# Input projection: x of chunks 1 to 3 read with channels on partitions and normed there, in place of transposes

## The reference

```python
x = layer_norm(x, ln0_g, ln0_b)         # over the 1024 channels of a frame
h = x @ w_in                            # 1024 -> 1408
a_val, a_gate = h[..., :384], h[..., 384:768]
p_in, q = h[..., 768:1152], h[..., 1152:]
a = a_val * jax.nn.sigmoid(a_gate)      # then a causal depthwise convolution of width 31
p = pool_mixer(p_in)                    # trailing means over 2, 4, 8, 16 frames
mo = memory_cross_attention(q, mem)
x = layer_norm(ALPHA * x + concat(a, p, mo) @ w_out, ln1_g, ln1_b)
```

## Time and profile before

| | us |
|---|---|
| Median of 3 runs | 1891.85 |
| Lowest and highest run | 1891.42, 1892.68 |
| The profiled execution | 1893.02 |
| its span in the trace | 1891.2 |
| TensorE busy in the span | 1844.0 |
| VectorE busy | 1503.3 |
| ScalarE busy | 935.3 |

### The profile page before, as it was taken

The page is one execution under the profiler, slowest core; times in us unless marked ns, Lnnn a source line. Parts: engine busy times, 40 slices in busy tenths (PEclk is TensorE's granted clock), DMA queues, the critical chain, the costliest instruction groups (busy, mean ns, idle before and its releaser), DMA issues.

```text
span 1891.2 us, 26166 instructions
## 1 busy us (share of the span) xinstructions
PE 1844.0 (98%) x8700; PEld 1537.0 (81%) x8700; DVE 1503.3 (79%) x1998; ACT 935.3 (49%) x1585; POOL 174.8 (9%) x250
## 2 busy tenths in 40 slices
PE   7999999999999999999999999999999999999998
PEld 7888888878887788888888788888888787888886
DVE  6636387899998888888888888787878868567999
ACT  3211125676665665656557665655557335325231
POOL 1201010000001022222220020000000000000111
PEclk9999999999999999999999999999999999999999
DMA  6533355444537434343436333122225658557543
GB/s 234 190 111 115 90 163 190 147 153 142 184 133 264 172 123 151 126 145 132 144 133 207 121 129 117 72 89 78 89 78 173 234 199 303 198 172 271 202 170 120
DMA packets 178074, 296.13 MB, mean 157 GB/s; under 512 B 11728, under 2 KB 112336, under 8 KB 178000
## 3 DMA queue, kind: packets, MB, share of 16 engines
q1 hardware_dynamic: 178000, 295.18, 45.1%
HBM read 189.19 MB, written 105.91 MB: 156 GB/s over the span
## 4 chain that ended last, share of the span: by engine, by line
PE 70%; DVE 9%; DMA 2%; ACT 2%; issue 2%; SPq 0%; POOL 0%; DVEq 0%; ACTq 0%; POOLq 0%
PE banks L2268 19%; PE banks L2265 19%; PE banks L2262 19%; PE banks L1199 6%; DVE mov_lo L2482 3%; DVE sta_lo L2478 1%; PE banks L1228 1%; DMA mov_raw<-x_operands 1%; PE banks L1181 1%; DVE up_and_out L2516 1%; DVE up_and_out L2513 1%; PE banks L1132 1%; PE banks L1152 1%; PE banks L1212 1%; PE banks L1263 1%
## 5 line engine op out<-in xcount | busy, mean ns | idle before, releaser
L2262 PE MATMUL banks<-mov_hi,sta_hi 128*128 128x512 f32 x1848 | 499.1, 391 | 6.7 <-ACT half_sums L2352 2.0
L2268 PE MATMUL banks<-mov_lo,sta_hi 128*128 128x512 f32 x1848 | 498.7, 390 | 4.0 <-DVE mov_lo L2482 3.6
L2265 PE MATMUL banks<-mov_hi,sta_lo 128*128 128x512 f32 x1848 | 497.7, 390 | 2.5 <-DVE sta_lo L2478 2.4
L2262 PEld LDWEIGHTS banks<-mov_hi,sta_hi 128*128 128x128 f32 x1848 | 346.4, 188 | 83.9 <-ACT half_sums L2352 3.6
L2268 PEld LDWEIGHTS banks<-mov_lo,sta_hi 128*128 128x128 f32 x1848 | 346.6, 188 | 80.1 <-DVE mov_lo L2482 8.6
L2265 PEld LDWEIGHTS banks<-mov_hi,sta_lo 128*128 128x128 f32 x1848 | 347.2, 188 | 76.3 <-DVE sta_lo L2478 4.1
L2332 ACT ACTIVATE sta_hi<-sta_raw 128x512 fp32r<-128x512 f32 (+1 forms) x340 | 197.7, 611 | 129.9 <-PE banks L2268 94.5
L2478 DVE TENSOR_TENSOR sta_lo<-sta_raw,sta_hi 128x512 fp32r<-128x512 f32 (+1 forms) x340 | 223.8, 673 | 34.6 <-ACT sta_hi L2332 32.7
L2361 ACT ACTIVATE half_sums<-banks 128x512 f32<-128x512 f32 x68 | 40.7, 598 | 175.9 <-PE banks L2268 175.9
L360 PE MATMUL banks<-x0t_hi,win_hi 128*128 128x512 f32 x320 | 126.5, 395 | 0.0
L360 PE MATMUL banks<-x0t_hi,win_lo 128*128 128x512 f32 x320 | 124.8, 390 | 0.0
(11 more groups left out here) (256 smaller groups left out, 2621.4 us busy)
## 6 DMA issues: line engine op xcount, KB each, us to landing
sta_raw<-in_w_up SPq DMA_DIRECT2D x88, 512.0 KB, 4.1
hidden_scratch<-up_and_out SPq DMA_DIRECT2D x44, 512.0 KB, 2.6
y_scratch<-up_and_out SPq DMA_DIRECT2D x16, 1024.0 KB, 7.3
sta_raw<-hidden_scratch SPq DMA_DIRECT2D x32, 512.0 KB, 4.6
up_and_out<-y_scratch SPq DMA_DIRECT2D x16, 1024.0 KB, 4.9
x_operands<-x_operands_out SPq DMA_DIRECT2D x56, 256.0 KB, 4.2
mov_raw<-x_operands SPq DMA_DIRECT2D x14, 1024.0 KB, 8.3
mov_raw<-in_w_down SPq DMA_DIRECT2D x44, 256.0 KB, 4.6
```

The source lines that it names most:

```text
L2262: pe.matmul(psum, sa_hi[j][:, k, :], mv_hi[j][:, k, :], start=(start and k == 0), stop=False, skip_group_check=True)
L2265: pe.matmul(psum, sa_lo[j][:, k, :], mv_hi[j][:, k, :], start=False, stop=False, skip_group_check=True)
L2268: last = pe.matmul(psum, sa_hi[j][:, k, :], mv_lo[j][:, k, :], start=False, stop=(stop and k == m - 1), skip_group_check=True)
```

## The change

Only chunk 0 is transposed on the chip. A second copy of x, `xT`, with channels first and frames in the kernel's order, is given to the kernel as an input. For chunks 1 to 3:

- Each tile is still loaded, normed with frames on partitions and stored. The mean and the root of each of its frames (two numbers, now side by side in columns 12 and 13 of the statistics) are stored too, to a new DRAM tensor of 2048 x 2 (`store_rows`).
- `load_turned` reads half `b` (four blocks of 128 channels) of the chunk from `xT`, 1 MB, into the buffer of the low part.
- When the four tiles of the chunk are stored, `load_rows` reads their 512 pairs back, spread to all 128 partitions.
- `normalise_turned`: VectorE subtracts the means and multiplies by the roots, each on 128 x 2048, in place. The second operand is repeated over the four blocks and steps by two words.
- `affine_hi`: ScalarE applies gain and shift, which are one number per partition here, block by block, and then rounds the half to the high part. It stands behind the evacuation of tiles 7 and 8 in chunk 0, 3 and 4 in chunk 1, 1 and 2 in chunk 2.
- `turned_lo`: VectorE subtracts the high part from the half in place.
- The first projection tile of a chunk waits for the low part of each half when it comes to it.

Slots of x are used in another order: after chunk 0 slot 3 holds the spread rows, and the other five go round. Tiles 4 to 6 are loaded right behind the weights; the loads, stores, norms and pool steps behind them are put in another order, with two more buffers for the pooling. SP waits for the stores of the first pooled half ahead of the load of the taps.

```diff
+    FIRST = 2 * TT
+    SLOTS = (0, 1, 2, 4, 5)
...
+    def slot_of(n):
+
+        return n if n < TT else SLOTS[(n - TT) % len(SLOTS)]
+
...
+    def splits(c, b):
+
+        return FIRST + 2 * (c - 1) + b + 1
...
+        xt_raw = [at("xT_rows0", 118784, [P, KT, CH]), at("xT_rows1", 49152, [P, KT, CH])]
...
+        gb_cols = at("ln0_gb_columns", 212672, [P, 2, KT])
+        row_stats = at("ln0_row_stats", 192512, [P, CH, 2])
...
-                if n in (4, 5):
+                slot = slot_of(n)
+                if n >= TT and slot >= TT and uses(n) == 1:
                     sp.wait_ge(win_lo, len(pieces))
-                if n >= RING:
-                    sp.wait_ge(x0_stored[n % RING], 16 * (n // RING))
-                    sp.wait_ge(tp_ready, 2 * (n - RING) + 2)
+                if uses(n) > 1:
+                    sp.wait_ge(x0_stored[slot], stores(slot, n - 1))
+                if slot < TT and uses(n) == 2:
+                    sp.wait_ge(tp_ready, 2 * slot + 2)
                 rows = a["x"][(n // 8) * HALF:(n // 8 + 1) * HALF, :].rearrange("(q r) d -> r q d", r=PHASES)[n % 8]
-                sp.dma_start(x0[:, n % RING, :], rows).then_inc(x_loaded[n % RING], 16)
+                sp.dma_start(x0[:, slot, :], rows).then_inc(x_loaded[slot], 16)
+
+            def load_turned(c, b):
+                if c >= 2:
+                    sp.wait_ge(proj, JT * (c - 1))
+                src = a["xT"][4 * b * P:4 * (b + 1) * P, c * CH:(c + 1) * CH].rearrange("(k p) t -> p k t", p=P)
+                sp.dma_start(xt_raw[c % 2][:, 4 * b:4 * b + 4, :], src).then_inc(xt_loaded[b], 16)
+
+            def store_rows(n):
+                sp.wait_ge(ln_rstd, n + 1)
+                sp.dma_start(rows_d[n * P:(n + 1) * P, :], st[:, n % RING, 12:14]).then_inc(x0_stored[slot_of(n)], 16)
+
+            def store_tile(n):
+                store_rows(n)
+                store_x0(n)
+
+            def load_rows(c):
+                for u in range(TT):
+                    n = c * TT + u
+                    sp.wait_ge(x0_stored[slot_of(n)], stores(slot_of(n), n))
+                if c == 1:
+                    sp.wait_ge(x0_stored[TT - 1], 16)
+                    sp.wait_ge(tp_ready, FIRST)
+                else:
+                    sp.wait_ge(xt_scaled, 2 * (c - 1))
+                src = rows_d[c * CH:(c + 1) * CH, :].rearrange("(o t) s -> o (t s)", o=1).to_broadcast((P, 2 * CH))
+                sp.dma_start(row_stats[:, :, :].rearrange("p t s -> p (t s)"), src).then_inc(rows_loaded, 16)
...
             load_x(4)
             load_x(5)
             load_x(6)
-            load_x(7)
+            for i, name in enumerate(("ln0_g_columns", "ln0_b_columns")):
+                sp.dma_start(gb_cols[:, i, :], a[name]).then_inc(cols_loaded, 16)
+            load_turned(1, 0)
+            load_turned(1, 1)
...
+                        sp.wait_ge(s, stored_of(i))
+                    sp.wait_ge(tp_ready, FIRST)
+                    sp.wait_ge(xt_scaled, 2 * (NCH - 1))
+                    for s in pooled_out:
+                        sp.wait_ge(s, 16)
...
+                if c == 0:
+                    store_tile(4)
+                    load_x(9)
+                    store_tile(5)
+                    load_x(10)
+                    store_gated(0, 0)
+                    load_x(7)
+                    load_x(8)
+                    store_tile(6)
+                    load_x(11)
+                    store_tile(7)
+                    load_rows(1)
+                    load_x(12)
+                    store_gated(0, 1)
+                    store_gated(0, 2)
+                    store_tile(8)
+                    load_x(13)
+                if c == 1:
+                    load_turned(2, 0)
+                    load_turned(2, 1)
+                    store_tile(9)
+                    load_x(14)
+                    store_tile(10)
+                    load_x(15)
+                    store_gated(1, 0)
+                    store_tile(11)
+                    load_rows(2)
+                    store_gated(1, 1)
+                    store_gated(1, 2)
+                    for n in range(12, 16):
+                        store_tile(n)
+                    load_rows(3)
                 if c == 2:
+                    load_turned(3, 0)
+                    load_turned(3, 1)
                     load_pool(0, 0)
-                for t in range(CT):
-                    store_x0((c + 1) * TT + t)
-                    store_gated(c, t)
-                    if c == 2 and t < 2:
-                        store_pooled(0, t)
-                        load_pool(0, t + 1)
-                store_x0((c + 1) * TT + 3)
-                if c + 2 < NCH:
-                    for u in range(TT):
-                        load_x((c + 2) * TT + u)
-                if c == 2:
+                    load_pool(0, 1)
+                    store_gated(2, 0)
+                    store_pooled(0, 0)
+                    load_pool(0, 2)
+                    store_gated(2, 1)
+                    store_pooled(0, 1)
+                    load_pool(0, 3)
+                    store_gated(2, 2)
                     store_pooled(0, 2)
-                    load_pool(0, 3)
                     store_pooled(0, 3)
...
-                pool.tensor_tensor(s[:, 14:15], s[:, 13:14], half[:, 0:1], ALU.pow).then_inc(ln_rstd, 1)
+                pool.tensor_tensor(s[:, 13:14], s[:, 13:14], half[:, 0:1], ALU.pow).then_inc(ln_rstd, 1)
...
-                if done == c * JT:
-                    pe.wait_ge(lo_done, 2 * TT * (c + 1))
+                if done == 4:
+                    pe.wait_ge(lo_done, FIRST)
...
+                    if c and done == c * JT and k % 4 == 0:
+                        pe.wait_ge(lo_done, splits(c, k // 4))
...
-                    for i in turns_behind(c, n):
-                        turn(c + 1, i)
...
+            def affine_hi(c, b):
+
+                n = 2 * (c - 1) + b + 1
+                act.wait_ge(xt_scaled, n)
+                act.wait_ge(cols_loaded, 32)
+                x = xt_raw[c % 2]
+                for k in range(4 * b, 4 * b + 4):
+                    last = act.activation(x[:, k, :], x[:, k, :], ACT.Identity, bias=gb_cols[:, 1, k:k + 1], scale=gb_cols[:, 0, k:k + 1])
+                last.then_inc(xt_affine, 1)
+                act.wait_ge(xt_affine, n)
                 if c >= 2:
                     act.wait_ge(proj, JT * (c - 1))
-                act.activation(xt_hi[c % 2][:, 4 * b:4 * b + 4, u * P:(u + 1) * P], turned(c, i).rearrange("p (k t) -> p k t", k=4), ACT.Copy).then_inc(hi_done, 1)
+                act.activation(xt_hi[c % 2][:, 4 * b:4 * b + 4, :], x[:, 4 * b:4 * b + 4, :], ACT.Copy).then_inc(hi_done, 1)
...
-                    for i in turns_behind(c, n):
-                        split_hi(c + 1, i)
+                    if c + 1 < NCH:
+                        for b in range(2):
+                            if n == (7, 3, 1)[c] + b:
+                                affine_hi(c + 1, b)
...
-                dve.scalar_tensor_tensor(out=x, in0=x, scalar=s[:, 14:15], in1=g_b[:, 1, :], op0=ALU.mult, op1=ALU.add).then_inc(x0_ready, 1)
-
-            def split_lo(c, i):
+                dve.scalar_tensor_tensor(out=x, in0=x, scalar=s[:, 13:14], in1=g_b[:, 1, :], op0=ALU.mult, op1=ALU.add).then_inc(x0_ready, 1)
...
+            def row_of(i):
+
+                return row_stats[:, :, i].rearrange("p (o t) -> p o t", o=1).to_broadcast((P, 4, CH))
+
+            def normalise_turned(c, b):
+
+                n = 2 * (c - 1) + b + 1
+                x = xt_raw[c % 2][:, 4 * b:4 * b + 4, :]
+                dve.wait_ge(xt_loaded[b], 16 * c)
+                dve.wait_ge(rows_loaded, 16 * c)
+                dve.tensor_tensor(x, x, row_of(0), ALU.subtract).then_inc(xt_centred, 1)
+                dve.wait_ge(xt_centred, n)
+                dve.tensor_tensor(x, x, row_of(1), ALU.mult).then_inc(xt_scaled, 1)
+
+            def turned_lo(c, b):
+                dve.wait_ge(hi_done, splits(c, b))
+                part = (slice(None), slice(4 * b, 4 * b + 4), slice(None))
+                dve.tensor_tensor(xt_lo[c % 2][part], xt_raw[c % 2][part], xt_hi[c % 2][part].bitcast(F32), ALU.subtract).then_inc(lo_done, 1)
...
             for c in range(NCH):
                 if c == 0:
+                    norms(1, 0)
                     gate(0, 0)
+                    norms(1, 1)
                     for i in range(7, 10):
                         weights_lo(i)
-                    norms(1, 0)
-                    norms(1, 1)
-                    lows(1, 0, 1)
+                    norms(1, 2)
                     gate(0, 1)
-                    norms(1, 2)
-                    lows(1, 2, 3)
                     gate(0, 2)
                     norms(1, 3)
-                    lows(1, 4, 5, 6, 7)
-                    continue
+                    norms(2, 0)
+                    for b in range(2):
+                        normalise_turned(1, b)
```

(81 more changed lines are left out.)

118 lines of the change are left out of this document (52 added, 66 removed).

## The result

The changed kernel takes 1900.01 us (median of 5 runs, 1897.63 to 1901.53) against 1891.85: a ratio of 1.0036, 95% interval 1.0025 to 1.0047. It is slower, by about 8 us. I had predicted 1888.8 us and a range of 1884.5 to 1894.0, so the forecast is wrong, in sign and in size. The profiled execution took 1901.53 us, span 1899.8.

A forecast was written before the change was run, and what follows sets the result against it. TensorE's stream was taken as the bound: +4.2 (chunk 1 starting later) - 7.8 (transposes for chunks 2 and 3) + 0.5 (clock) = -3.1 us, giving 1888.8 us, -0.16%; range 1884.5 to 1894.0.

The forecast's parts named there:

- the one on DRAM: Chunk 1's way through DRAM: tile 7 ready at 67.1, store 2.7 us, spread 3.8, with issue rows at 73.8.
- from the rows to the first tile: Chunk 1: from rows at 73.8 through norming, affine and low parts to the first projection tile's end at 94.2.
- its own terms: Range terms: tile 4's bounds (-1.8, +1.7), the transfers (-0.8, +2), the clock (-0.5, +2).
- Rival 3: Chunk 1: tile 7 comes 5.3 us late behind stores of 5.6 us in a full queue; sum +2.2, 1894; chance 0.14.
- Some 20 us of slack each: Chunks 2 and 3: low parts end by 129 and 175, TensorE asks at about 148 and 208; 7.8 us kept.
- The 3.6 us of chunk 0: Transposes removed from four projection tiles of chunk 0: 25.36 us become 21.76, so it ends at 81.0.
- the 7.74 behind chunk 1's first tile: Transposes for chunks 2 and 3 removed from TensorE: 3.9 + 3.9 = 7.8 us gained.
- Rival 2: normalise_turned's stepped operand is read at half rate, 4.5 us per operation, not 2.3: +4.2, 1896; chance 0.08.
- The clock: TensorE's 4.7 us wait at chunk 1 most likely drops its clock to about 0.50, 1.2 GHz; costs 0.5 us.
- the second wait: TensorE's wait for chunk 1's second low half, 88.4 to 91.5; a slow first half, to 90.8, is hidden by it.

The follow-up runs named there:

- e1: Changed kernel without the stores of row statistics, the spread loading the same 4 KB from vector g: 1891.93 us, 0.9993 of the kernel before.
- e3: Changed kernel with each 1 KB row store written as 2 pieces of 512 bytes, from g: 1892.67 us, 0.9997 of the kernel before.
- n1: Order of e2, spread of e1, row stores of 128 pieces of 512 bytes from g: 1890.88 us, 0.9989 of the kernel before.
- n2: Order of e2, spread of e1, row stores of 128 pieces of 64 bytes from g: 1890.33 us, 0.9983 of the kernel before.
- e2: Changed kernel with only SyncE's order in chunk 0 moved, tiles 7 and 8 loaded earlier, 11 later: 1892.03 us, 0.9993 of the kernel before.
- e4: Changed kernel with the edits of e1 and e2 together: 1887.35 us, 0.9973 of the kernel before.
- g2: Changed kernel with chunk 1's rows spread by TensorE, statistics of tiles 5 to 7 and loads of 7 and 8 early: 1904.09 us, 1.0055 of the kernel before.
- g3: Changed kernel, still through DRAM, with tiles 5 to 7's statistics and 8-byte row stores early, tile 7 loaded first: 1906.25 us, 1.0073 of the kernel before.
- g1: Order of e2, spread of e1, 8-byte row stores ahead of the tiles' stores on a semaphore no load waits for: 1893.81 us, 1.0002 of the kernel before.
- h2: Kernel e2 with the 8-byte row stores issued by ScalarE on its own queue, with own semaphores: 1891.83 us, 0.9994 of the kernel before.
- h3: Kernel e2 with each 8-byte row store behind its tile's store, on a semaphore only the spread waits for: 1893.54 us, 1.0000 of the kernel before.

## Why the prediction was wrong

**The step that failed** is the one on DRAM: "The store of tile 7 (the row statistics go out ahead of it, covered by its last norm steps) takes 2.7 us", and with it "At 2.7 us a store tile 7 lands about 62, just before VectorE asks for it at 62.5. I count no delay". I priced the row stores at nothing, by the moment at which they are issued, and took the tile's store from an empty queue. From the trace after: tile 7 is normed 5.7 us late (72.8 for 67.1), its store goes out 1.9 later still, because SyncE stands at the load of tile 11 (I had 0.2 for all issuing, so +1.7), the store takes 7.3 for 2.7 (+4.6), and the spread 5.0 with its issue for 3.8 (+1.2). That makes up the 13.2 us by which the rows are late; from the rows to the first tile it is 20.2 us, forecast 20.4. e1, e3, n1 and n2 show that the stores in 8-byte pieces make the store of a tile slow, e2 that SyncE's order adds to it, e4 that nothing else was missing for chunk 1. By what means 8-byte pieces do this stays open. The range could not have held this: its own terms, added to 1888.8, give 1885.7 to 1894.5 (not quite the 1884.5 to 1894.0 stated), with 2 us for all transfers.

**Rival 3** named the right place and its wait (5.3 us forecast, 5.78 measured), with the wrong cause, a full queue, which is the smaller part: in e1, which keeps the loads, VectorE waits 1.36 us for tile 7. That its number came out is in part luck: the two stores held SyncE for 6.1 and 7.3 us, not 5.6 each. It let only the tile's lateness count and not the slow store of tile 7 itself, so it stopped at 1894.

**A rule I didn't weigh.** The Trainium skill (DMA: Bandwidth & Descriptors, Specifications) puts the least size for full rate at 512 bytes and says that smaller transfers are read, modified and written; it speaks against this change. The runs agree in so far as stores in 8-byte pieces cost (6.2 us for the store of tile 7 in e2 against 3.1 in e4); at 64 bytes, also below that size, they show no such cost (3.1 in n2), and no run here shows the reading and writing back. By that rule the store of tile 7 would not have been priced from rows of large transfers alone.

**"Some 20 us of slack each"** was wrong for chunk 2 by the same step: its rows were forecast at 111 and came at 138. (Chunk 3's were forecast by 158; VectorE began them at 189.6, when their xT had landed, and TensorE did not wait.) g2 shows that chunk 2 then costs a wait of 10.8 us as soon as chunk 1 is on time. So making chunk 1 early, with the row stores of chunk 2 left as they are, would not have saved the change (g2, g3).

**What held.** The 3.6 us of chunk 0 (TensorE's wait begins at 99.0 - 18.0 = 81.0, as forecast) and the 7.74 behind chunk 1's first tile. Rival 2 is false: 2.29 us for an operand with a step of two words. The Trainium skill (SBUF — State Buffer, Door 1: The DMA port swizzle) had it so, and the trace agrees. The clock: 0.56 on average over TensorE's wait, 0.50 at 102 to 103, which is 1.2 GHz, and back at 1.00 at 104. As forecast, the slow half tile hid the second wait: 12 matmuls took 5.1 us, from 99.0 to 104.1, when the second low half was done (101.82 + 2.29). In e4, where TensorE waited 5.1 us, close to the 4.7 of the prediction, the granted clock was 0.50 too from 84 to 90, and 0.2 us were left of the second wait.

## What to carry to other kernels

A transfer of 1 KB in 8-byte pieces was not small here: don't price such a one at nothing for its few bytes, look at the size of its pieces and at what else is moving then. Where a queue's next entry waits for a landing, price every store by the slowest landing in that stretch, not by one from an empty queue. When a chain is mended, follow the same mechanism into the next stage before counting the gain; a delay upstream hides it.

## What was unexpected of the hardware

- Beside stores of 128 pieces of 8 bytes, 512 KB stores landed in 6.0 to 7.5 us (medians of five in e2 and g1, in h2 with the small pieces on another engine's queue, in h3 with them issued behind the tile), against 4.1 to 4.3 in e4, n1 and n2, without them or with pieces of 64 or 512 bytes. Whether it is the size itself, the place that the pieces are read from, or that several pieces lie close together in DRAM was not tried; no run here separates them.
- In e2 the slow store moved its bulk at 300 to 400 GB/s and then dripped for 2 us at under 20 GB/s. Which engine or piece is late, the trace doesn't show.
- A column of 128 numbers, repeated as the stationary operand against the identity, is spread to all partitions by TensorE at 1.95 us for 8 such columns, less than the 7.1 + 4.9 us of the store and the spread by way of DRAM in the changed kernel.
